# Gates, convolution, q/k maps and the two transforms of the second block's mixer, spread over three stages instead of a stage of their own

## What is computed

```python
u = rmsnorm(h, mix_norm[i]) @ w_in[i]
c_q, c_kv, k_rope, m_x, m_v, m_o, m_if, f_in = split_cols_2(u, IN_SPLITS)
y = jnp.concatenate([mla_mixer(...), mlstm_mixer(...), fnet_mixer(f_in, ...)], axis=-1)
h = h + y @ w_out[i]

# mlstm_mixer
xc = jax.nn.silu(conv(m_x, conv_w, 5 taps) + conv_b)
q, k = xh @ w_q, xh @ w_k                      # a 64x64 map for each head
i_pre, f_pre = g[:, :, 0] + i_bias, g[:, :, 1] + f_bias
# mlstm_chunkwise, forward and (flipped) backward; lf = log_sigmoid(f_pre)
b = jnp.cumsum(lfc); D = where(causal, b_t - b_s + ic_s); m_t = running maximum
s = (q @ k.T) * exp(D - m_t)
h = (s @ v) / maximum(abs(sum(s)), exp(-m_t))
out = (norm(h_fwd + h_bwd) * head_norm + skip * xc) * sigmoid(m_o)

# fnet_mixer
y = fftn(zg, axes=(positions, channels)).real  # as matrices: channels, then positions
return einsum(y, w) + b
```

## Time and profile before

| | us |
|---|---|
| median of three runs | 3755.55 (3752.52 to 3756.9) |
| the profiled execution's own time | 3755.55 |
| its span | 3753.8 |
| gates stage, layer 0 and layer 1, first matmul to the core's first | 37.57 and 35.01 |
| core stage, layer 0 and layer 1, first matmul to the next stage's first | 59.68 and 59.67 |

### The profile page before, as it was taken

The page is one execution under the profiler, slowest core; times in us unless marked ns, Lnnn a source line. Parts: engine busy times, 40 slices in busy tenths (PEclk is TensorE's granted clock), DMA queues, the critical chain, the costliest instruction groups (busy, mean ns, idle before and its releaser), DMA issues. The chain is left out here.

```text
span 3753.8 us, 41947 instructions
## 1 busy us (share of the span) xinstructions
PE 3546.1 (94%) x15638; PEld 2790.2 (74%) x15654; DVE 1600.5 (43%) x2127; ACT 1333.6 (36%) x1864; POOL 510.6 (14%) x414
## 2 busy tenths in 40 slices
PE   8999999998899998999998899999999998899998
PEld 6777688866668886888864678886888774578885
DVE  3386433355553334333356733325333346733335
ACT  3343322235632224332324533225332324533324
POOL 0001211010221101221000022102221000022202
PEclk9999999999999999999999899999999999899999
DMA  4201233221023321333210123313333220123322
GB/s 139 84 1 40 68 100 103 93 68 62 23 73 95 102 100 56 98 99 104 82 52 29 51 84 99 113 63 96 95 97 110 78 65 29 41 83 99 105 81 73
DMA packets 77743, 294.16 MB, mean 78 GB/s; under 512 B 8624, under 2 KB 11184, under 8 KB 77360
## 3 DMA queue, kind: packets, MB, share of 16 engines
q1 hardware_dynamic: 77616, 292.45, 24.4%
HBM read 290.32 MB, written 2.10 MB: 78 GB/s over the span
## 5 line engine op out<-in xcount | busy, mean ns | idle before, releaser
L146 DVE TENSOR_TENSOR w_low<-w_raw,w_high 128x1024 fp32r<-128x1024 f32 (+4 forms) x513 | 672.8, 1311 | 1567.2 <-ACT w_high L141 1567.2
L180 PE MATMUL bank<-x_high,w_high 128*128 128x512 f32 x2856 | 1128.5, 395 | 74.6 <-POOL x_low L224 22.0
L181 PE MATMUL bank<-x_low,w_high 128*128 128x512 f32 x2856 | 1119.2, 392 | 0.0
L182 PE MATMUL bank<-x_high,w_low 128*128 128x512 f32 x2856 | 1118.8, 392 | 0.0
L141 ACT CAST w_high<-w_raw 128x1024 fp32r<-128x1024 f32 (+4 forms) x513 | 554.9, 1082 | 866.6 <-PE bank L182 861.3
L180 PEld LDWEIGHTS bank<-x_high,w_high 128*128 128x128 f32 x2856 | 540.7, 189 | 207.3 <-issue 36.6
L182 PEld LDWEIGHTS bank<-x_high,w_low 128*128 128x128 f32 x2856 | 540.7, 189 | 113.8
L181 PEld LDWEIGHTS bank<-x_low,w_high 128*128 128x128 f32 x2856 | 541.3, 190 | 112.4 <-issue 2.2
L180 PE MATMUL bank<-hidden_high,w_high 128*128 128x512 f32 x1056 | 410.8, 389 | 0.0
L181 PE MATMUL bank<-hidden_low,w_high 128*128 128x512 f32 x1056 | 410.8, 389 | 0.0
L182 PE MATMUL bank<-hidden_high,w_low 128*128 128x512 f32 x1056 | 410.8, 389 | 0.0
(11 more groups left out here) (499 smaller groups left out, 3659.8 us busy)
## 6 DMA issues: line engine op xcount, KB each, us to landing
w_raw<-in_stream SPq DMA_DIRECT2D x381, 512.0 KB, 3.5
w_raw<-in_stream SPq DMA_DIRECT2D x96, 704.0 KB, 4.0
w_raw<-in_stream SPq DMA_DIRECT2D x16, 384.0 KB, 3.1
dft_positions<-in_dft SPq DMA_DIRECT2D x2, 2048.0 KB, 7.4
w_raw<-in_stream SPq DMA_DIRECT2D x4, 576.0 KB, 3.7
h<-in_x SPq DMA_DIRECT2D x8, 256.0 KB, 6.0
w_raw<-in_stream SPq DMA_DIRECT2D x16, 128.0 KB, 2.1
out<-result SPq DMA_DIRECT2D x4, 512.0 KB, 2.7
```

Of the source, the lines that this page charges most:

```text
L146: self.nc.vector.tensor_tensor(self.lo[:, j % 2, 0:size], self.raw[:, j % RAW_SLOTS, 0:size], self.hi[:, j % 2, 0:size].bitcast(F32), ALU. ...
L180: nc.tensor.matmul(out, lhs[0], rhs[0], start=start, stop=False)
L181: nc.tensor.matmul(out, lhs[0], rhs[1], start=False, stop=False)
L182: return nc.tensor.matmul(out, lhs[1], rhs[0], start=False, stop=stop)
```

## The change

The gates stage is gone; its work is spread over three stages.

- **In-stage.** The job of k_rope and the gates comes as job 5 instead of 11 (the stream is packed so, and `tile_of` gives its tile). Gate copies, biases, logarithm, convolution, scans, Silu, Sigmoid and the split of v run on ACT, DVE and POOL between the jobs. The rotation table's parts move from jobs 6 to 9 to jobs 6, 7, 10, 11.
- **Attention stage** (`mla_stage`). After each of the first 15 units PE does a side task in bank 5 or 7: four channel transforms, four q maps, two k maps, the small transposes, four spreads. The attention's product with v has bank 4 alone and its output transposes bank 6 alone. ACT and DVE take the side tasks out. The stage ends with `keep_warm`.
- **Core stage** (`mlstm_stage`). SP issues the 2 MB `dft` and the group weights at its start. One matmul of the position transform follows each of the steps 2 to 9 (group 1) and 12 to 19 (group 0), the group maps follow steps 23 and 26. The step order becomes key block by key block, both directions; products go to banks 0 and 1 by turns. The diagonal block of direction 1 gets a gate exponent of its own in bank 3, so there are 16 more pick matmuls of 128 columns and 12 more exponentials.

```diff
@@ second_in_stage, ACT
+                    if j == gates_job + 1:
+                        nc.scalar.copy(kr[0:HD, :], prj[0:HD, 11, :]).then_inc(S.k_copied, 1)
...
+                        nc.scalar.activation(M.gi, prj[64:64 + G, 11, :], ACT.Copy).then_inc(S.gates_in, 1)
+                        nc.scalar.activation(M.lf, prj[96:96 + G, 11, :], ACT.Copy).then_inc(S.gates_in, 1)
+                    if j == gates_job + 3:
+                        act.wait_ge(S.biased, 2)
+                        nc.scalar.activation(M.gw, M.lf, ACT.Abs).then_inc(S.mag, 1)
...
+                        nc.scalar.activation(M.gw, M.gw, ACT.Ln, bias=1.0).then_inc(S.log_ready, 1)
...
+                    if j == 13:
+                        act.wait_ge(S.conv_done, 2)
+                        nc.scalar.activation(M.xc, M.xc, ACT.Silu).then_inc(S.conv_ready, 1)
+                    if j == uq:
+                        nc.scalar.activation(prj[:, 7:9, :], prj[:, 7:9, :], ACT.Sigmoid).then_inc(S.sigmoid_done, 1)
+                    if j == uq + 1:
...
+                            nc.scalar.copy(hi[:, :, :, half], src).then_inc(S.v_high, 1)
@@ second_in_stage, POOL
+                pool.wait_ge(S.multiplied, 13 + 3)
+                for v_part, x in ((M.v_hi, 1.0), (M.v_lo, 0.0)):
...
@@ second_in_stage, DVE
+                    if j in (mix_in + 2, mix_in + 3):
+                        convolve(j - mix_in - 2)
...
+                    if j in (11, 12):
+                        scan_gates(j - 11)
@@ mla_stage, PE
+                for n in range(N + 3):
...
+                    m = n - 2
+                    if 0 <= m < N:
+                        pe.wait_ge(S.turned_used, m + 1)
+                        if m:
+                            pe.wait_ge(S.normed, m)
...
+                            mm = nc.tensor.matmul(C.bank[4][:, 0:P],
...
+                    if 0 <= n - 1 < tasks:
+                        task(n - 1)
+                keep_warm(nc, C, C.bank[0], 8)
@@ mlstm_stage
+    steps = [(h, d, b) for h in range(ML_HEADS) for b in range(NB) for d in range(2)]
+    POS = {1: 2, 0: 12}
+    Y, OUT, END = {1: 11, 0: 21}, {1: 23, 0: 26}, {1: 25, 0: 28}
...
+                sp.dma_start(dft[:, :, :, :], C.dft_dram).then_inc(S.dft_in, 16)
+                sp.dma_start(fw, C.small_dram[:, first:first + 2, :]).then_inc(S.dft_in, 16)
...
+                def fnet(s):
+                    for g in (1, 0):
+                        k = s - POS[g]
+                        if 0 <= k < 2 * NB:
+                            if k == 0:
+                                pe.wait_ge(S.dft_in, 32)
...
+                            mm = nc.tensor.matmul(C.bank[2][:, :], M.z(k // 2, g)[:, k % 2 * P:(k % 2 + 1) * P],
+                                                  dft[:, k % 2, k // 2, :], start=k == 0, stop=k == 2 * NB - 1)
...
                 for s, (h, d, b) in enumerate(steps):
...
-                    if s % U == first_turn[b]:
-                        if h:
-                            pe.wait_ge(S.weighted, U * (h - 1) + last_turn[b] + 1)
+                    if d == 0:
+                        if s >= 4:
+                            pe.wait_ge(S.weighted, s - 2)
...
+                    diagonal = C.bank[3 if d else 4][:, key]
+                    if d:
+                        nc.tensor.matmul(diagonal, pick, ga_parts[:, d, key], start=True, stop=False,
+                                         skip_group_check=True)
...
                     if s >= 3:
                         accumulate(s - 3)
+                    fnet(s)
@@ mlstm_stage, ACT
+                        if d:
+                            if b:
+                                nc.scalar.activation(ww[:, 1, lo:b * P], C.bank[5][:, lo:b * P], ACT.Exp, bias=column)
+                            lo = b * P
```

More of the change, by code:

```diff
@@ new lines, in task @@
+                def task(k):
+                    bank = side_bank(k)
+                    if Q <= k < K:
+                        act.wait_ge(S.mapped, k - Q + 1)
+                        nc.scalar.activation(M.q_hi[:, k - Q, :], bank[:, :], ACT.Copy,
+                                             scale=HD ** -0.5).then_inc(S.q_high, 1)
+                    if K <= k < COLS:
+                        act.wait_ge(S.mapped, ML_HEADS + k - K + 1)
+                        for i in range(2):
+                            nc.scalar.copy(M.k_pair[0:HD, 2 * (k - K) + i, :],
+                                           bank[HD * i:HD * (i + 1), :]).then_inc(S.k_high, 1)
+                    if LEAST <= k < tasks:
+                        act.wait_ge(S.spread, k - LEAST + 1)
+                        nc.scalar.activation(M.least[k - LEAST], bank[:, :], ACT.Exp,
+                                             scale=-1.0).then_inc(S.least_ready, 1)
@@ new lines, in _ @@
+                for n in range(N + 4):
+                    if n < N:
+                        act.wait_ge(S.bias_ready, n + 1)
+                        if n >= 2:
+                            act.wait_ge(S.turned, n - 1)
+                        nc.scalar.activation(probs[:, n % 2, :], C.bank[n % 2][:, :], ACT.Exp,
+                                             bias=bias[:, n:n + 1], scale=scale,
+                                             accum_out=total[:, n:n + 1]).then_inc(S.exp_done, 1)
+                    if n < 2:
+                        act.wait_ge(S.parts_zero, n + 1)
+                        dst, src, done = ((gm_parts, M.gm, S.gm_high) if n else (ga_parts, M.ga, S.ga_high))
+                        nc.scalar.copy(dst[0:G, :, :], src).then_inc(done, 1)
+                    task(n - 2)
+                    m = n - 4
+                    if m >= 0 and units[m][1] == MLA_HEADS - 1:
+                        qb = units[m][0]
+                        act.wait_ge(S.o_turned, qb + 1)
+                        nc.scalar.copy(mix[:, 0:HALF_T, qb * P:(qb + 1) * P],
+                                       C.bank[6][:, :].rearrange("p (f q) -> p f q", q=P)).then_inc(S.o_used, 1)
@@ L2438, in accumulate @@
                         pe.wait_ge(S.den_in, 2 * (h - 1) + d + 1)
-                    mm = three(nc, C.bank[6 + d][:, lo:hi], (v_hi[:, b, h, :], v_lo[:, b, h, :]),
-                               (w_hi[:, m % 4, lo:hi], w_lo[:, m % 4, lo:hi]), i < 2, i >= U - 2)
-                    mm.then_inc(S.block_used, 1)
+                    out, high, low = C.bank[6 + d][:, lo:hi], w_hi[:, m % 4, lo:hi], w_lo[:, m % 4, lo:hi]
+                    nc.tensor.matmul(out, v_hi[:, b, h, :], high, start=i < 2, stop=False, skip_group_check=True)
@@ L2479, in _ @@
                         h, d, b = steps[s]
-                        lo, hi = span(d, b)
                         act.wait_ge(S.gated, s + 1)
```

598 lines of the change are left out of this document (332 added, 266 removed).

## The result

The changed kernel took 3737.61 us (median of 4 runs, 3735.54 to 3740.98), the kernel before 3755.28 us (3752.52 to 3756.9) beside it: a ratio of 0.9947, 95% interval 0.9936 to 0.9959, so 17.7 us or 0.5% less. The forecast was 3739.5 us. The profiled execution has a span of 3733.6 us against 3753.8, 20.2 us less.

What follows compares the result with a forecast made beforehand. TensorE bounds the kernel. Gates stage gone, -72.6 us, plus 2 x (in-stage 0.5 + attention 13.4 + core 14.4) gives -16.0, from 3755.55 to 3739.5 us; range 3724 to 3762.

Steps and rivals of the forecast that it cites:

- What bounds the kernel: Whole kernel: TensorE, busy 94% of the span; only its idle or half-clock time can be won.
- In-stage, +0.5: In-stage: no matmul added, moved work fits beside TensorE; +0.5 us a layer, between 0 and 2.
- Attention, +13.4: Attention stage: TensorE has no room, so side tasks count in full; +13.4 us a layer.
- The second rival: Attention side tasks paced by DVE and ACT: +20 us, 3759.5; both no-change cases together had chance 0.20.
- Core, work 52.3: Core: matmul work at full clock, 32.5 plus transform 16.6 plus picks 3.2, together 52.3 us a layer.
- The matrix, idle 5.5: Core's start: matrix takes 8.0 us, TensorE reaches the wait after some 2.5; idle 5.5 us.
- The divisions, 4.5: Core's third head: waits behind DVE's divisions fall from 8.6 to 4.5 us.
- Borders 1: Core: waits at the heads' borders become 1 us.
- Half clock 7: Core: half clock's price, 12.5 us before, becomes 7, between 3 and 20; keep_warm should save the first head's share.
- the slower rival: Core: half clock keeps its share of the work, 20 us, 13 more a layer; 3766 us, chance 0.14.
- The third rival: Core: transform beside nothing, division waits stay 8.6, clock costs 9: +6 a layer, 3751.5; both no-change cases 0.20.
- The faster case: Core fills up: clock cost 3, division waits 2, so 6.5 us a layer less; 3726.5 us, chance 0.12.

Runs made afterwards that it cites:

- order_alone: Kernel before with only the core's new inner order of blocks, two product banks and 16 extra picks: 3754.23 us, ratio 0.9994.
- no_transform: Changed kernel without the core's 16 position matmuls, 2 maps and their 4 evacuations, matrix still fetched: 3713.37 us, ratio 0.9887.
- no_warm_end: Changed kernel without the 8 dummy matmuls at the attention stage's end: 3738.56 us, ratio 0.9948.
- combined: Changed kernel, transform three steps later, 6 dummy matmuls before the first accumulation, POOL's subtractions for v moved to the attention stage: 3727.19 us, ratio 0.9914.
- late_start: Changed kernel with the core's position transform, its copies and maps three steps later: 3729.68 us, ratio 0.9928.
- filled_wait: Changed kernel with 24 dummy matmuls in front of the core's wait for the matrix: 3734.70 us, ratio 0.9942.
- matrix_in_four: Changed kernel with the 2 MB matrix fetched in four transfers, each with its own wait, as has the small map: 3733.35 us, ratio 0.9934.
- combined_pool: combined with the third head's two products with the inverse and its sum on POOL instead of VectorE: 3725.19 us, ratio 0.9907.

## Why the prediction was right, step by step

- **What bounds the kernel** held: the gain is TensorE's idle time in the stages that I named.
- **In-stage, +0.5.** Right: +0.38 in layer 1. Of the nine profiled kernels with this in-stage, all take 118.2 or 118.3 us in layer 1, and in layer 0 six take 118.2 or 118.3 and three 119.2 or 119.3. The 1.47 of the changed kernel is one of these three: 1 us of it is a longer stretch of half clock at the stage's end, which the old in-stage shows as well (119.3 in layer 0 of order_alone). The remaining 0.35 us have their place where I looked for them, POOL beside DVE near jobs 15 and 16.
- **Attention, +13.4.** Right at +13.2 and +12.8. A unit of the kernel before takes 3.39 us, one with a channel transform 4.26 and one with a spread 4.01 (lines below; a map costs as much as a transform). That gives 10 x 0.87 + 4 x 0.62 and 0.7 for the small transposes, 11.9 for the side tasks (11.5 forecast). Add 1.1 for keep_warm (1.3) and 0.6 for the wait between the last two products with v (0.6), and it is 13.6, 0.4 more than layer 0's 13.2. TensorE has 70.31 us of matmuls in 72.29, so DVE and ACT pace nothing. The second rival, +1 us for each evacuation, is out. PE's timeline of the kernel before, two units' starts:

```profile
1962.66 1.02 PE L2161 MATMUL bank<-mla_k,mla_q 128*128 128x512 f32 x2
1966.05 1.02 PE L2161 MATMUL bank<-mla_k,mla_q 128*128 128x512 f32 x2
```

And of the changed kernel, two channel transforms and two spreads, each a unit apart:

```profile
1963.01 1.03 PE L2343 MATMUL bank<-consts,projections 128*128 128x256 f32 x4
1967.27 1.03 PE L2343 MATMUL bank<-consts,projections 128*128 128x256 f32 x4
...
2002.17 0.49 PE L2365 MATMUL bank<-w_low,latent_low 40*128 40x512 f32 x1
2006.18 0.50 PE L2365 MATMUL bank<-w_low,latent_low 40*128 40x512 f32 x1
```

- **Core, work 52.3.** 52.6 and 51.7. The picks' 3.2, taken between 1 and 7, is 3.2 by order_alone and 2.4 by no_transform; the transform's 16.6 is 17.5 and 16.6 against no_transform's 35.1.
- **The matrix, idle 5.5.** 5.43 and 5.53. The size is right, its source was misread: the rows of the gates stage name `fnet_weights`, a small load behind the matrix, as what ended the wait. The trace has the matrix landed 7.5 us after its issue in layer 0 and 7.3 in layer 1, and the transform starts 9.0 and 8.1 us after the stage does. My 8.0 for the matrix came out because in the changed kernel again a small load behind it, landed 8.0 us after the core's start, ends the wait. That is luck.
- **The divisions, 4.5.** 3.07 + 0.33 + 0.24 = 3.6 in layer 0, 3.07 + 1.48 = 4.6 in layer 1. The reason given has two parts, and the experiments separate them: the order takes 8.6 to 6.1 (order_alone), the transform's matmuls the rest.
- **Borders 1.** None is left. The rest, 1.5: 2.2 in layer 0 (0.32 and 0.52 for ACT's copies out of bank 2, 0.30 + 0.18 + 0.28 + 0.63 at the core's end), 1.7 in layer 1.
- **Half clock 7.** 6.5 and 7.2. The size was right, one reason wrong, so that the size is in part luck: I had keep_warm save the first head's share. It saves hardly anything in front of an 8 us transfer, since TensorE's 2.5 us of work there is hidden at either clock (no_warm_end), and it costs 1.1 us. What saves the clock is the transform among the other matmuls (no_transform: 14.4 us without it). I took that only as a denser list, without a number. The kernel before had shown the first point. PE's timeline, the gates stage of layer 1:

```profile
3149.66 5.14 PE L2187 MATMUL bank<-consts,projections 128*128 128x256 f32 x16 [1.39 <-PEq L64]
```

Here half clock lay ahead of the wait, 5.14 us instead of layer 0's 3.69 for the same matmuls, and the transform started no later for it. So the 2.97 us of idle time, which I counted against the slower rival as being followed by no half clock, had half clock in front of them.
- **The slower rival**, half clock as a share of the work, would have been 20 us a layer. It asked what a longer core costs at the old rate; the longer core changed the rate.
- **The third rival**, the transform in series with 8.6 us of division waits, has the first half right (the work adds in full) and the second wrong.
- **The faster case**, a core that fills up, is what combined reaches, by another way: the division waits are still 4.1 us, but the matrix is waited for only 1.1, the half clock costs 3.4 and 2.1, and the core is 6.4 and 7.9 us shorter. late_start's is 7.5 and 3.7 us shorter.

**What stays open**: why the clock stays at half for 16.7 us of running matmuls in no_transform and 9.2 us in one layer of late_start, and comes back after some 6 us in the changed kernel. The runs show that the transform's matmuls among the others shorten it and that dummies ahead keep it from starting, not which property of them counts. To wait for the matrix alone in front of the transform, and for the small map behind step 23, would save 0.7 us a layer in the changed kernel, an estimate from the landings above; no run tried it by itself. To fetch the matrix in the attention stage already would remove the 5.4 us at their root. That wasn't tried: its 16 KB a partition are given out only when q, k and v are released, and whether there is room earlier stays open.

## What to carry to other kernels

Merging a stage of waits into dense neighbours is priced by the idle time it holds, and each moved matmul counts in full as work; here the longer list of matmuls gave part of it back by the clock, which no term of the forecast had. A transfer that is issued at the start of the stage that needs it is still waited for after the merge, so place its first user by the transfer's time, not by the loop's convenience, and let each load have its own wait: read in the profile which load ended a wait for several. Twenty-four dummy matmuls in the wait for the matrix won 3.2 us a layer (filled_wait), and six kept the clock up where a wait of 1.23 us had let it fall (combined); in front of work that a transfer hides, eight were worth nothing (no_warm_end).

## What the runs showed of the hardware that I had not expected

- A PE that the profile shows as busy can stay at half clock: 16.70 us with a matmul running for 16.70 of them, at a mean clock of 0.52 (no_transform). A wait of 1.23 us was followed by half clock (late_start), one of 3.07 us in the changed kernel as well, while 1.30 us in combined and 2.97 us in the kernel before were followed by none.
- A transfer of 2 MB in one piece had landed 7.3 us after its issue (the changed kernel). In four pieces (matrix_in_four) the first had landed after 4.9 us and the others 7.0, 8.3 and 9.7 us after the first one's issue.
- Each of POOL's three operations in combined_pool made one DVE operation with two SBUF inputs longer (0.41 to 1.43, 0.28 to 0.78, 0.68 to 1.23 us), and only one; those with one input in PSUM kept their times.
